# A hybrid decoder step on one core: the first two expert units expert by expert, ring places freed one by one, zero products ahead of the last up

## The chip, the cores and the metric

The kernel runs on one core of one Trainium2 chip. The metric is the device time of one execution in microseconds (us), given as the median of several runs. The engines are named as in the profile: PE (TensorE, the matrix products), PEld (its weight loads), DVE (VectorE), ACT (ScalarE), POOL (GpSimd) and SP (SyncE, which here only issues DMAs). DMAs are issued on three queues, those of SP, ACT and POOL, and are carried by the same 16 DMA engines.

## The reference

One inference step of a one-layer decoder, all in float32, for a prompt of 512 tokens and 8 decode tokens of width 1024. Two groups of attention heads (stick-breaking and NSA) read one input projection, are normalised and go through an output projection into the residual x. Behind them stands the part that matters here, a mixture of experts:

```python
def hierarchical_moe(h, ...):                       # h: 520 rows of 1024
    g_idx = argmax(group logits)                    # one of 4 groups
    top_w, top_i = lax.top_k(softmax(expert logits of that group), 2)
    expert_id = g_idx * 4 + top_i                   # two of 16 experts per row
    gate = einsum('nd,edf->nef', h, w_gate)         # 1024 -> 512 for each expert
    up   = einsum('nd,edf->nef', h, w_up)
    act  = silu(gate) * up * combine                # combine is zero for experts not chosen
    return einsum('nef,efd->nd', act, w_down)       # 512 -> 1024
# then: output = rms_norm(x + moe(rms_norm(x)), norm_final)
```

Each of the 16 experts has three weight matrices of 2 MB (gate, up, down), 96 MB in all.

## The kernel before

**Rows by expert.** The kernel computes for each expert only the rows that chose it. The normalised rows are written to DRAM (h_rows), each row gets a slot in a table, and the rows of an expert are gathered from DRAM by an indirect DMA on POOL, turned on PE, and multiplied by the expert's weights. Work is cut into 16 units (`UNITS`). Units 0 and 1 are special: they hold rows of experts 1 and 2 (`FIXED`), of which 64 rows each are known before the last tile of the prompt (unit 0) and 32 rows each come with the last tile (unit 1). Units 2 to 15 are one expert each with 32 to 128 rows, in an order of experts that is computed on the chip (`order_i`) and read by SP into registers.

**A unit's steps.** On PE: gate products (8 blocks of K, `gate_or_up(j, 0)`), up products, the turning of the activations (`transpose_acts`), down products (`finish_down`), and between them the rows of the next unit (`rows_of`). On ACT: exp of the gate, the copies of the turned rows and activations, the copy of the output (`y_out`) and its store (`store_rows`). On DVE: the rest of silu (`gated`), the product with up (`times_up`), half of the copies. The two units use separate banks for gate and up (`hidden_to`). Behind unit 2's up, DVE also computes where each row's results will lie (`extra_blocks`, `place_results`), a chain of small operations.

**The stream of weights.** 48 loads of 2 MB (`CHUNKS`) go through a ring of 8 places (`RING`, `homes`). SP issues them in the order of `CHUNKS`: gate 0, gate 1, up 0, up 1, down 0, down 1, gate 2, up 2 (the first eight, at fixed points of the plan, as soon as the attention part no longer needs the space), then gate 3, up 3, down 2, gate 4, up 4, down 3 and so on. The eight first ones are issued in the order 0, 1, 3, 4, 2, 5, 6, 7. Load n of the ring waits until load n - 8 has been used, by a count that PE raises at the end of a whole gate, up or down (`e_gate`, `e_up`, `e_down`). Since units 0 and 1 both read experts 1 and 2, the counts wait for unit 1 for both places (`max(j, 1) + 1`). In this text "gate 7" is the load or the product group of unit 7. A DMA that stands in SP's queue behind a waiting one waits too.

**The plan.** A recording layer writes the kernel as a list of steps (`PLAN`), and each engine takes its own steps in that order. In the attention part the order comes from times in units that `place(time, step)` gives (`agenda`); behind it the order is written out by hand. `fill(n)` puts n of the 16 steps of unit 0's gate products between the last steps of routing on PE.

**The output.** The results of experts go to DRAM (`expert_rows`), those of units 14 and 15 stay on chip. For each of the five tiles (order `SUM_ORDER`: 0, 4, 1, 2, 3; 4 is the tile of 8 decode rows) DVE adds the two gathered rows to x (`add_rows`, two operations, the second writes into a pair of PSUM banks that PE has "opened" with products of zeros), PE adds the late units' rows by products with selection matrices, ACT takes squares and the root, DVE scales (`scaled`), and SP stores. There are three pairs of banks (`final_banks`): tiles 0 and 2 share banks 3 and 4, tile 3 and the decode tile share 6 and 7, tile 1 has 0 and 1. So tile 2 must wait for tile 0's scaling and tile 3 for the decode tile's.

## Time and profile before

| what | us |
|---|---|
| median of 3 runs (753.1 to 756.13) | 754.16 |
| the profiled execution | 759.51 |
| its span, from the first to the last instruction | 757.7 |
| PE busy | 699.8 |
| DVE busy | 343.3 |
| ACT busy | 215.9 |
| mean granted clock of TensorE | 0.973 of full |

The span covers all but 1.8 us of the profiled execution, and this execution is 5.4 us longer than the median. Times in the rows are us from the start of the span. A row of the timeline gives start, length, engine, line, operation, tile written and tiles read, count; in square brackets stands how long the engine was idle before it and what it then waited for. Rows that end in "xN" merge N instructions. Before about 250 us lie the input projection and the decode tokens, up to some 465 us the prompt's attention, and from there the experts.

### The profile page before, as it was taken

Reading aid. Unit: us, or ns where it says so; the run is one execution under the profiler, and the core shown is the slowest. Engines: PE = TensorE matmul, PEld = TensorE weight load, DVE = VectorE, ACT = ScalarE, POOL = GpSimd, SP = SyncE. Lnnn points to the kernel's source line nnn. Section 1 sums busy time; section 2 is a strip of 40 time slices with the busy share of each in tenths; the row PEclk is TensorE's granted clock in tenths of the full one; section 3 lists DMA queues with packets and bytes.
Section 4 is the critical chain, followed back from the end, with each engine's and each line's share of the span. In section 5 each row is a group of like instructions: output and inputs, shape, how many; then the busy total and the mean of one; then the engine's idle time right before and its main releaser. Section 6 shows DMA issues by size and latency. Waiting matters only on the chain.

```text
span 757.7 us, 13582 instructions
## 1 busy us (share of the span) xinstructions
PE 699.8 (92%) x5251; PEld 385.2 (51%) x5251; DVE 343.3 (45%) x770; ACT 215.9 (28%) x557; POOL 125.4 (17%) x174
## 2 busy tenths in 40 slices
PE   7878999999999989979989999999899999989885
PEld 3446456444554445545545665745554664565331
DVE  6411103595222455665775665606634253123245
ACT  1111111112211555657657831011010110101103
POOL 0111100120000443142253241110010000100050
PEclk9998999999999989999999999999999999999988
DMA  8265891667757530000000069999999999999982
GB/s 290 72 181 158 237 395 44 230 233 231 230 175 209 202 132 1 1 3 1 1 29 1 1 221 384 309 383 396 365 396 397 395 408 398 376 404 408 410 288 112
DMA packets 101491, 172.55 MB, mean 228 GB/s; under 512 B 22893, under 2 KB 40653, under 8 KB 101394
## 3 DMA queue, kind: packets, MB, share of 16 engines
q1 hardware_dynamic: 79682, 142.83, 52.6%
q10 hardware_dynamic: 18656, 20.35, 7.9%
q0 software_dynamic: 3088, 8.49, 3.2%
q8 instruction: 43, 0.70, 0.4%
q14 instruction: 22, 0.18, 0.1%
HBM read 151.78 MB, written 22.98 MB: 231 GB/s over the span
## 4 chain that ended last, share of the span: by engine, by line
PE 70%; issue 9%; DVE 7%; DMA 6%; ACT 4%; SPq 2%; POOL 2%; DVEq 0%; ACTq 0%; POOLq 0%
PE bank L2701 15%; PE bank L3168 13%; PE bank L1998 7%; PE bank L2731 6%; PE bank L3151 6%; PE bank L1915 3%; PE bank L1936 3%; DMA reg<-w_up 3%; DMA reg<-w_gate 3%; PE bank L1794 2%; PE bank L1949 2%; SPq L2211 2%; PE bank L3172 1%; PE bank L1917 1%; DMA x<-x_prompt 1%
## 5 line engine op out<-in xcount | busy, mean ns | idle before, releaser
L3168 PE MATMUL bank<-reg 128*128 128x512 f32 (+1 forms) x352 | 148.4, 568 | 0.8 <-DMA reg<-w_in 0.4
L2701 PE MATMUL bank<-reg,qreg 128*32 128x128 f32 (+2 forms) x1264 | 109.2, 336 | 6.6 <-DMA reg<-w_up 3.9
L3168 PEld LDWEIGHTS bank<-reg 128*128 128x128 f32 x352 | 65.3, 194 | 59.3 <-issue 55.5
L2701 PEld LDWEIGHTS bank<-reg,qreg 128*32 128x32 f32 (+2 forms) x1264 | 66.3, 126 | 47.8 <-issue 30.6
L1280 POOL TENSOR_SCALAR reg<-reg,st,gates 128x128 f32<-128x128 f32 (+3 forms) x64 | 41.2, 652 | 185.2 <-DVE st L1568 185.1
L3151 PE MATMUL bank<-cf,reg 128*128 128x128 f32 (+1 forms) x384 | 61.9, 280 | 10.0 <-DVE rt L1759 4.9
L1998 PE MATMUL bank<-reg 128*128 128x512 f32 x128 | 62.7, 613 | 0.4 <-DVE x L1680 0.3
L3151 PEld LDWEIGHTS bank<-cf,reg 128*128 128x128 f32 (+1 forms) x384 | 41.9, 142 | 30.2 <-issue 24.0
L3002 ACT ACTIVATE work<-bank 128x128 f32<-128x128 f32 (+5 forms) x107 | 40.8, 411 | 49.2 <-PE bank L3151 47.8
L2731 PE MATMUL bank<-reg,work 128*32 128x256 f32 (+1 forms) x368 | 47.5, 476 | 1.1 <-ACT work L2353 0.7
L1564 DVE TENSOR_REDUCE st<-bank 128x2 f32<-128x256 f32 (+3 forms) x32 | 26.3, 822 | 41.8 <-PE bank L1917 41.7
L3106 DVE COPY work<-bank 128x128 f32<-128x128 f32 (+4 forms) x55 | 22.8, 429 | 49.3 <-PE bank L3151 49.3
L2292 POOL DMA_INDIRECT work<-h_rows,ids x14 | 13.6, 969 | 176.6 <-PE bank L2744 128.1
L1395 ACT ACTIVATE reg<-bank,st 128x128 f32<-128x128 f32 (+3 forms) x64 | 33.2, 524 | 28.8 <-DVE st L1564 28.6
L1936 PE MATMUL bank<-work,vreg 128*64 128x128 f32 x480 | 38.0, 289 | 2.0 <-DVE work L3106 2.0
L2969 POOL TENSOR_TENSOR reg<-reg,cf 128x128 f32<-128x128 f32 (+5 forms) x30 | 15.4, 533 | 146.7 <-ACT reg L3059 138.8
L2459 DVE TENSOR_SCALAR work<-work 128x256 f32<-128x256 f32 (+3 forms) x16 | 5.4, 335 | 74.6 <-ACT work L2348 74.6
L1936 PEld LDWEIGHTS bank<-work,vreg 128*64 128x64 f32 x480 | 26.0, 139 | 24.3 <-issue 21.8
L2460 DVE RECIPROCAL work<-work 128x256 f32<-128x256 f32 (+3 forms) x16 | 36.0, 2253 | 0.6
L2361 ACT COPY work<-bank 128x512 f32<-128x512 f32 (+1 forms) x16 | 8.9, 558 | 78.8 <-PE bank L2731 58.5
L1998 PEld LDWEIGHTS bank<-reg 128*128 128x128 f32 x128 | 22.1, 193 | 16.8 <-issue 15.8
L2731 PEld LDWEIGHTS bank<-reg,work 128*32 128x32 f32 (+1 forms) x368 | 16.9, 122 | 26.3 <-issue 20.3
(374 smaller groups left out, 921.9 us busy)
## 6 DMA issues: line engine op xcount, KB each, us to landing
reg<-w_gate SPq DMA_DIRECT2D x13, 2048.0 KB, 19.2
reg<-w_down SPq DMA_DIRECT2D x12, 2048.0 KB, 20.3
reg<-w_up SPq DMA_DIRECT2D x11, 2048.0 KB, 18.3
reg<-w_in ACTq DMA_DIRECT2D x16, 512.0 KB, 6.6
expert_rows<-vreg SPq DMA_DIRECT2D x14, 512.0 KB, 6.9
vreg<-w_up SPq DMA_DIRECT2D x3, 2048.0 KB, 18.8
reg<-cache_sb_k SPq DMA_DIRECT2D x16, 256.0 KB, 4.5
reg<-cache_sb_v SPq DMA_DIRECT2D x16, 256.0 KB, 3.9
```

What stands on the lines that cost most here:

```text
L1280: ins = G.tensor_scalar(prob, prob, w[:, e:e + 1], gate[:, e:e + 1], ALU.mult, ALU.mult)
L1395: nc.scalar.activation(prob_of(key, e)[:, 0:n], at(ring, key)[:, 0:n], ACT.Exp, bias=st[:, top:top + 1], accum_out=st[:, col:col + 1]).the ...
L1564: V.tensor_reduce(st[:, top:top + 2], psum[:, 2:4, 0:n], AX.X, ALU.max, negate=True).then_inc(sg["arg"], 1)
L1936: ins = T.matmul(to[64 * e:64 * e + 64, :], v, probT[:, turn_at[key] % 3, e, k * P:(k + 1) * P], start=(k == 0 and b != WIN), stop=(k == i ...
L1998: ins = T.matmul(at(ring, ("wout", i, group))[0:r, :], chunks_of(i)[:, part, 0:r], w_out[group // 2][:, k, 512 * half:512 * half + 512], s ...
L2460: link_loop(V.reciprocal(s_, s_), 3 * j + 2)
L2701: ins = T.matmul(to[rows, at_:at_ + w], rowsT[b][:, k, r0:r0 + n], w_[:, k, h * w:(h + 1) * w], start=(k == 0), stop=(k == KD - 1))
L2731: ins = T.matmul(to[rows, at_:at_ + w], actsT[j % 2][:, 4 * r0 // P + k % per, q:q + n], w_[:, k, w * h:w * h + w], start=(k == 0), stop=( ...
L3002: ins = nc.scalar.activation(dst, src, ACT.Copy, scale=scale)
L3106: ins = nc.vector.tensor_copy(dst, src)
L3151: ins = nc.tensor.transpose(dst, src, ident[0:src.shape[0], 0:src.shape[0]])
L3168: ins = nc.tensor.matmul(at("m", ("proj", n))[:, 0:w], hT[:, k, i * P:(i + 1) * P], win[:, pos % 2, k, 0:w], start=(k == 0), stop=(k == KD ...
```

## The change

Four things change.

1. **The order of loads.** Up 1 (load 3) is placed in the agenda, ahead of the store of h rows behind which it stood. Up 2 (load 7) is split: 4 and 2 of its 8 K blocks go right behind gate 2, the remaining 2 at the old place. Down 2 now stands ahead of gate 3 in the ring, and a table `USED` tells which load's place each load takes (`HOME`).
2. **Units 0 and 1.** Unit 1's gate products (`late_gate`) go into the middle and the end of unit 0's (`fill(6)`, expert 1's block of unit 1, `fill(4)`, expert 2's block), up and down go expert by expert over both units, and the counts rise by one after each expert of unit 1, so that a place is freed as soon as both units have used it (`freed`). Unit 0's counts rise at the end of unit 0 (`finished(0)` is 2). The order of experts is computed behind the gates. Unit 1's down products go to bank 1, its activations are turned in the middle of the downs, and the turns of unit 2's rows stand between the last two down blocks.
3. **Zero products.** Ahead of the last up (up 15), PE does ten products of zeros into the banks of tile 0.
4. **The output.** Four pairs of banks (tile 0: 6 and 7, tile 1: 4 and 5, tile 2: 2 and 3, decode tile: 0 and 1): only tile 3 waits for a pair, tile 0's, and this wait stands on PE ahead of tile 2's products. DVE adds four tiles before the first scaling. Two pairs are opened before down 15 and two behind it.

On SP the order of DMAs around the attention's end, before and after (`h2_rows` is the store of h rows, in brackets what a DMA waits for; `L1256` and `L1266`, `L2211` and `L2239` or `L2242` are the same line in both):

```order
L1256 DMA h2_rows<-reg1 128x1024 [waits h2] x2
L2211 DMA qreg<-w_up 128x8x512 [waits z_full]
L2211 DMA reg0<-w_down 128x4x1024 [waits t_full]
L1256 DMA h2_rows<-reg1 128x1024 [waits h2]
L2211 DMA vreg<-w_up 128x8x512 [waits st_v,pv]
L2211 DMA reg0<-w_down 128x4x1024 [waits m_full]
L2211 DMA reg1<-w_gate 128x8x512 [waits m_full]
L2211 DMA reg1<-w_up 128x8x512 [waits st_h2,e_rowsT_full]
```

```order
L1266 DMA h2_rows<-reg1 128x1024 [waits h2]
L2239 DMA qreg<-w_up 128x8x512 [waits z_full]
L1266 DMA h2_rows<-reg1 128x1024 [waits h2]
L2239 DMA reg0<-w_down 128x4x1024 [waits t_full]
L1266 DMA h2_rows<-reg1 128x1024 [waits h2]
L2239 DMA vreg<-w_up 128x8x512 [waits st_v,pv]
L2239 DMA reg0<-w_down 128x4x1024 [waits m_full]
L2239 DMA reg1<-w_gate 128x8x512 [waits m_full]
L2242 DMA reg1<-w_up 128x4x512 [waits squares]
L2242 DMA reg1<-w_up 128x2x512
L2242 DMA reg1<-w_up 128x2x512 [waits st_h2,e_rowsT_full]
L2239 DMA reg1<-w_down 128x4x1024 [waits e_gate]
```

Up 1 (`qreg<-w_up`) moves past one store, up 2 (`reg1<-w_up`) comes in three pieces, and a down (down 2) stands ahead of the read of the order.

On PE the first two units, from the last 16 fill rows (`64x256` into `L2050`/`L2060` are unit 0's gate) to the first down block, before and after. `32x128` are unit 1's blocks, `64x256` unit 0's:

```order
L2050 MATMUL bank<-reg0,qreg 64x256 x15
L2676 MATMUL bank<-gain,token 1x16 [waits turns,x_dve]
L2701 MATMUL bank<-reg1,qreg 32x128 [waits z_dve,o_act,ga_act,t_dve,gb_act,e_rows_a,m_dve,e_rows_v,slot0]
L2701 MATMUL bank<-reg1,qreg 32x128 x31
L2701 MATMUL bank<-reg0,qreg 32x128 [waits slot1]
L2701 MATMUL bank<-reg0,qreg 32x128 x31
L2701 MATMUL bank<-vreg,qreg 64x256 [waits slot2]
L2701 MATMUL bank<-vreg,qreg 64x256 x15
L2701 MATMUL bank<-qreg 64x256 [waits slot3]
L2701 MATMUL bank<-qreg 64x256 x15
```

```order
L2060 MATMUL bank<-reg0,qreg 64x256 x7
L2711 MATMUL bank<-reg1,qreg 32x128 [waits o_act,z_dve,t_dve,ga_act,gb_act,m_dve,e_rows_a,e_rows_v]
L2711 MATMUL bank<-reg1,qreg 32x128 x31
L2060 MATMUL bank<-reg0,qreg 64x256 x8
L2711 MATMUL bank<-reg0,qreg 32x128 x32
L2727 MATMUL bank<-gain,token 1x16 [waits turns,x_dve]
L2711 MATMUL bank<-vreg,qreg 64x256 [waits o_act,t_dve,z_dve,ga_act,m_dve,gb_act,slot2]
L2711 MATMUL bank<-vreg,qreg 64x256 x15
L2711 MATMUL bank<-vreg,qreg 32x128 x32
L2711 MATMUL bank<-qreg 64x256 [waits slot3]
```

Unit 1's gates have moved into and behind unit 0's, ahead of the product that gives the order (`gain,token`), and unit 1's up of an expert follows unit 0's of the same.

Further on PE, from the first turning of activations to unit 2's gate (`64x512` is a down block of unit 0, `32x256` one of unit 1, `cf,work 128x128` are turns):

```order
L2707 MATMUL bank<-cf,work 128x128 [waits e_act]
L2707 MATMUL bank<-cf,work 128x128 x3
L2731 MATMUL bank<-reg0,work 64x512 [waits slot4,e_actT]
L2731 MATMUL bank<-reg0,work 64x512 x7
L2731 MATMUL bank<-reg0,work 64x512 [waits slot5]
L2731 MATMUL bank<-reg0,work 64x512 x7
L2707 MATMUL bank<-cf,work 128x128 [waits e_act]
L2707 MATMUL bank<-cf,work 128x128
L2683 MATMUL bank<-cf,work 128x128 [waits e_x0]
L2683 MATMUL bank<-cf,work 128x128 x7
L2731 MATMUL bank<-reg0,work 32x256 [waits e_y_v,slot4,e_y_a,e_actT]
L2731 MATMUL bank<-reg0,work 32x256 x15
```

```order
L2758 MATMUL bank<-cf,work 128x128 [waits e_act]
L2758 MATMUL bank<-cf,work 128x128 x3
L2781 MATMUL bank<-reg0,work 64x512 [waits e_actT,slot4]
L2781 MATMUL bank<-reg0,work 64x512 x7
L2758 MATMUL bank<-cf,work 128x128 [waits e_act]
L2758 MATMUL bank<-cf,work 128x128
L2781 MATMUL bank<-reg0,work 32x256 [waits e_actT]
L2781 MATMUL bank<-reg0,work 32x256 x15
L2781 MATMUL bank<-reg0,work 64x512 [waits slot5]
L2781 MATMUL bank<-reg0,work 64x512 x7
L2734 MATMUL bank<-cf,work 128x128 [waits e_x0]
L2734 MATMUL bank<-cf,work 128x128 x7
```

Unit 1's turns and its first down block stand between unit 0's two down blocks, with a wait for ACT's copy (`e_actT`) that nothing separates from the turns.

The diff, cut to its core:

```diff
-OPEN_FIRST = (0, 4, 1)
+OPEN_FIRST = (0, 4)
 CHUNKS = [("gate", 0), ("gate", 1), ("up", 0), ("up", 1), ("down", 0), ("down", 1), ("gate", 2), ("up", 2)]
-CHUNKS += [(w, j - (w == "down")) for j in range(3, 15) for w in ("gate", "up", "down")]
+CHUNKS += [("down", 2), ("gate", 3), ("up", 3)]
+CHUNKS += [(w, j - (w == "down")) for j in range(4, 15) for w in ("gate", "up", "down")]
 CHUNKS += [("gate", 15), ("down", 14), ("up", 15), ("down", 15)]
+USED = list(CHUNKS)
+USED[RING:RING + 3] = [("gate", 3), ("up", 3), ("down", 2)]
+HOME = {key: n for n, key in enumerate(CHUNKS[:RING])}
+for n, key in enumerate(CHUNKS[RING:]):
+    HOME[key] = HOME[USED[n]]
...
+    place(SHARE * (REP * 2 + 5) + 269, step, "chunk", 3)
     for _, _, f, args in sorted(agenda):
         f(*args)
-    for n in (3, 4):
-        step("chunk", n)
+    step("chunk", 4)
...
-    step("chunk", 7)
+    step("chunk_part", 7, 1)
     use("x", ("count",), "dve")
     step("count")
     sg.mark("turns", 0)
-    fill(10)
+    fill(6)
+    step("late_gate", 0)
+    fill(4)
+    step("late_gate", 1)
...
+        elif kind == "late_gate":
+            e, = key
+            if e == 0:
+                acquire_all(pe)
+                pe.wait_ge(sg["e_rows_a"], 1)
+                pe.wait_ge(sg["e_rows_v"], 1)
+            two_blocks(1, 0, e).then_inc(sg["e_gate"], 1)
...
-        n = (3, 0, 3, 6, 6)[i]
+        n = (6, 4, 2, 6, 0)[i]
...
+    def finished(j):
+
+        return j + 2
+
+    def freed(j):
+
+        return j + 2 if j else 1
...
             for n in range(RING, len(CHUNKS)):
+                before, j = USED[n - RING]
+                if CHUNKS[n] == ("gate", 3):
+                    sg.wait(sp, "x_dve", ("order",))
                 if CHUNKS[n][0] == "gate":
                     next_expert(CHUNKS[n][1])
-                before, j = CHUNKS[n - RING]
-                sp.wait_ge(sg["e_" + before], max(j, 1) + 1)
+                sp.wait_ge(sg["e_" + before], freed(j))
                 load_chunk(sp, n, expert_reg[CHUNKS[n][1]])
...
-            for i in (0, QT, 1):
+            for i in (0, QT, 1, 2):
                 add_rows(i)
             sg.wait(dve, "gain_in", "final")
             scaled(0)
-            add_rows(2)
-            scaled(QT)
             add_rows(3)
-            for i in range(1, QT):
+            for i in (QT, 1, 2, 3):
                 scaled(i)
...
+            wait_chunk(pe, "up", 0)
+            two_blocks(0, 1, 0)
+            two_blocks(1, 1, 0).then_inc(sg["e_up"], 1)
+            wait_chunk(pe, "up", 1)
+            two_blocks(0, 1, 1).then_inc(sg["e_up"], 1)
             sort_ids()
-            gate_or_up(1, 1, sg["e_up"])
+            two_blocks(1, 1, 1).then_inc(sg["e_up"], 1)
             pe.wait_ge(sg["e_act"], 1)
             transpose_acts(0, 4, sg["e_actT_full"])
-            finish_down(0)
+            wait_chunk(pe, "down", 0)
+            pe.wait_ge(sg["e_actT"], 1)
+            down_block(0, 0)
             pe.wait_ge(sg["e_act"], 2)
             transpose_acts(1, 4 * UNITS[1] // P, sg["e_actT_full"])
+            pe.wait_ge(sg["e_actT"], 2)
+            down_block(1, 0).then_inc(sg["e_down"], 1)
+            wait_chunk(pe, "down", 1)
+            down_block(0, 1).then_inc(sg["e_down"], 1)
             rows_of(2)
-            finish_down(1)
+            down_block(1, 1).then_inc(sg["e_down"], 1)
...
+                if j == 2:
+                    pe.wait_ge(sg["e_y_a"], 2)
                 gate_or_up(j, 1, sg["e_up"])
...
+            pe.wait_ge(sg["picked"], TILES)
+            for _ in range(5):
+                zero_banks(0, True, True)
             gate_or_up(LAST, 1, sg["e_up"])
...
+            for i in (1, 2):
+                open_banks(i).then_inc(sg["late_full"], 1)
             for i in SUM_ORDER:
                 to = final_banks(i)
-                if i not in OPEN_FIRST:
-                    sg.wait(pe, "final", (0, QT)[i - 2])
-                    open_banks(i).then_inc(sg["late_full"], 1)
+                if i == 2:
+                    sg.wait(pe, "final", 0)
+                    open_banks(3).then_inc(sg["late_full"], 1)
```

## Rows read from the trace of the kernel before

**Rows 1.** Page, its span and the DMA share in 40 slices (tenths).
```profile
span 757.7 us, 13582 instructions
...
DMA  8265891667757530000000069999999999999982
```

**Rows 2.** Windows: length, busy us of PE to POOL, clock, DMA share, GB/s.
```profile
480.00:540.60 60.60, 56.73 (x552) 32.19 (x542) 32.41 (x86) 5.94 (x12) 5.52 (x6) 1.00 1.04 377
540.60:673.70 133.10, 133.10 (x1363) 75.24 (x1363) 47.99 (x86) 15.56 (x35) 8.61 (x9) 1.00 1.04 395
673.70:735.50 61.80, 53.42 (x482) 27.87 (x480) 17.29 (x21) 5.58 (x13) 9.92 (x10) 0.92 1.00 384
```

**Rows 3.** Timeline of SP's queue, 370 to 560 us.
```profile
383.98 57.15 SPq L1256 DMA_DIRECT2D h_rows<-reg  x2
441.17 0.43 SPq L2211 DMA_DIRECT2D qreg<-w_up  x1
...
476.07 0.37 SPq L2211 DMA_DIRECT2D reg<-w_up  x1
...
483.29 0.39 SPq L2211 DMA_DIRECT2D reg<-w_gate  x1
...
552.21 0.37 SPq L2211 DMA_DIRECT2D reg<-w_gate  x1
```

**Rows 4.** Line L2211's issue to landing: whole span; 430-480; 514-560; down 15.
```profile
DMA to landing us min/median/max: 9.3/19.9/25.8
...
DMA to landing us min/median/max: 10.5/13.2/14.6
...
DMA to landing us min/median/max: 16.0/18.3/21.0
...
reg<-w_down SPq DMA_DIRECT2D x1, 2048.0 KB, 25.4
```

**Rows 5.** Timeline of PE, 428 to 500 us.
```profile
429.40 0.29 PE L1917 MATMUL bank<-cb 128*128 128x128 bf16 x2
...
474.77 4.54 PE L2050 MATMUL bank<-reg,qreg 128*64 128x256 f32 x40
...
479.37 3.70 PE L2701 MATMUL bank<-reg,qreg 128*32 128x128 f32 x128
...
495.34 7.09 PE L2731 MATMUL bank<-reg,work 128*64 128x512 f32 x32 [0.68 <-ACT work L2353]
```

**Rows 6.** Timeline of PE at unit 4's gate.
```profile
540.59 5.56 PE L2701 MATMUL bank<-qreg 128*64 128x256 f32 x96 [2.60 <-DVE qreg L2451]
```

**Rows 7.** Timeline of PE, units 13 to 15.
```profile
675.80 7.23 PE L2701 MATMUL bank<-reg,qreg 128*64 128x256 f32 x96 [2.09 <-DMA reg<-w_gate]
...
683.43 5.56 PE L2701 MATMUL bank<-reg,qreg 128*64 128x256 f32 x96
...
699.09 3.67 PE L2701 MATMUL bank<-vreg,qreg 128*64 128x256 f32 x32
...
704.76 5.52 PE L2731 MATMUL bank<-qreg,work 128*64 128x512 f32 x48 [1.36 <-DMA qreg<-w_down]
...
714.72 3.65 PE L2731 MATMUL bank<-reg,work 128*64 128x512 f32 x16 [0.46 <-DMA reg<-w_down]
722.24 5.36 PE L2701 MATMUL bank<-reg,qreg 128*64 128x256 f32 x32 [3.87 <-DMA reg<-w_up]
...
728.56 1.65 PE L2661 MATMUL bank<-cb,wr 32*128 32x512 bf16 x6
730.15 5.35 PE L2731 MATMUL bank<-reg,work 128*64 128x512 f32 x16
```

**Rows 8.** Output: line L2634's first and last start; timeline of PE and DVE.
```profile
L2634 DVE SCALAR_TENSOR_TENSOR x<-reg,weight,x x4: 1264/1272/1286, 729.6 to 744.9; 128x1024 f32<-128x1024 f32 x4
...
743.89 1.95 PE L2840 MATMUL bank<-work,cf 64*128 64x512 f32 x4 [1.45 <-DVE bank L2638]
...
753.28 1.28 DVE L2644 SCALAR_TENSOR_TENSOR x<-bank,small,gain 128x1024 f32<-128x1024 f32 x1 [1.42 <-ACT small L2416]
```

94 lines of the change are left out of this document (60 added, 34 removed).

## The prediction

> **What bounds the kernel now.** The page comes first, for the shares: PE is at 92%, and the DMA row stands at 9 from the 25th slice on in all but the last two [rows 1]. Both look full there, so the windows tell which one is: from 480 to 735 us the 16 DMA engines are busy all the time (share 1.00 to 1.04, 377 to 395 GB/s), while PE has no gap at all from 540.6 to 673.7 and gaps of 8.4 us in 673.7 to 735.5 [rows 2]. So the expert weights (48 loads of 2 MB, in one fixed order on SP's queue) and PE run side by side, both full in the middle, and the stream of loads decides at the end: PE waits 2.09 us for gate 13, 1.36 for down 13, 0.46 for down 14 and 3.87 for up 15 [rows 7], 7.8 of the 8.4 together. Two of these waits are followed by products at half clock: 96 products take 7.23 us after the first and 5.56 otherwise, 32 take 5.36 after the last and 3.67 otherwise, and the last down takes 5.35 where down 14's like group took 3.65 [rows 7]. Then 22.2 us of output sums follow up to 757.7, in which DVE and PE take turns [rows 1, 8].
>
> Then the start of the stream. SP stands from 383.98 to 440.80 on a store of h rows, and up 1 goes out only behind it, at 441.17 [rows 3], although the score products whose end it waits for ended at 429.7 [rows 5]. Up 2 goes out at 476.07, gate 3 at 483.29. And how long a load takes: 10.5 to 14.6 us from 430 to 480, where the queue is short, 16.0 to 21.0 from 514 to 560, where others stand ahead of it; the least of all, gate 1's at the start on idle engines, was 9.3 [rows 4].
>
> **Part 1: loads earlier.** Up 1 goes ahead of the store: 429.8 instead of 441.17. Up 2 goes in three pieces: 1.5 MB waits only for the squares of the last tile's mixture, long done when SP comes from gate 2 (about 465), and 0.5 MB waits for what all of it waited for, 476.07. What is queued on SP behind that wait, down 2, isn't ready sooner anyway. Down 2 takes gate 0's place, which is free after 12 of the 16 fill steps and unit 1's gate block of expert 0: fills cost 0.45 us each and the block 1.85 [rows 5], so 474.77 + 2.7 + 1.9 = 479.4, against 483.29 for the first load from the ring before. Gate 3 needs the order, which now comes behind all gates: 483.1 + 0.2 and the register load, about 484.7. Up 3 goes at 488.9, gate 4 at 494.2, up 4 at about 502, down 3 at about 508.
>
> What is that worth? A load lands at the later of two times: 5.1 to 5.9 us behind the one ahead of it (395 GB/s with the stores and gathers between), or its issue plus the time that a load alone takes. Followed so, the stream stands 8 to 10 us earlier at units 3 and 4. But a place comes free only when PE has used it, and PE isn't earlier. The tightest point is gate 7: it was issued at 552.2, right when its place came free, and landed 16.0 us later, the least in [rows 4] for this stretch. Alone it needs 9.3 to 13.2 us (ends: the shortest of all, and the median before 480). I take 10, nearer to the low end, because before 480 stores and indirect transfers stood between, and 0.7 for PE's own delay (part 2): 16.0 - 10 - 0.7 = 5.3, with the loads around it at 5 to 7. Behind that the engines are full again and can't catch up, so **the end of the stream moves by 5.5 us** (2 to 8): up 15 from 722.2 to 716.7, down 15 (issued at 703.9, 25.4 us) from 729.3 to 723.8 [rows 4, 7].
>
> The Trainium skill (DMA: Bandwidth & Descriptors, Anatomy of one DMA) fits a DMA as 2.0 us plus its bytes at 436 GB/s, 6.8 us for 2 MB, for the gpsimd path. The shortest of this trace is 9.3, on SP's queue; by the page's figure the stream would move by 8.5 us, and the second rival below would be the likeliest.
>
> **Part 2: the first two units.** The same products in another order. Gates, ups and turns add to the same 474.77 to 494.01, since no load is waited for (down 0 and 1 landed long before). Then down of unit 0, expert 0 (3.55), turns of unit 1 (0.4), and here is a new wait: ACT must copy these turns before unit 1's down can start. The same hand-over for unit 0 costs PE 0.68 us with a copy of 512 columns [rows 5]; with 256 columns I take 0.5. Before, it was covered by the rows of unit 2. Another 0.2 for the rest: **PE is 0.7 us late** at unit 2 (0.3 to 1.2). Unit 0's exponential and gating come some 2 us later on ACT and DVE; up of both experts is done at 492.4, DVE is free by then, and PE wants its result at 494.0. DVE's long chain of placing results starts behind up 2 and ends at 540.59, where PE waits 2.60 us for it [rows 6]; it moves with PE, so the 0.7 isn't absorbed there. The gather for unit 2 starts 2 us later and its rows are wanted at 505. Up 2 also waits for unit 1's output to be copied out of its bank: ACT gets there behind unit 0's stores, at 510, and PE comes at 515. The branch for more rows stays untaken.
>
> **Part 3: the end of the experts.** PE reaches gate 13 at 673.7 + 0.7 = 674.4; it has landed at 670.2. No wait, and full clock: from there to down 13 PE needs the 27.6 us of before less the lost 1.7, so down 13 starts at 700.3 and ends at 705.8 instead of 710.3. Down 14 ends at 713.4. Ten zero products take 0.21 to 0.27 us each (six take 1.65 in [rows 7]): 2.6 us at most, up to 716.0. They lie in the wait for up 15, which lands at 716.7; cover gone, they would cost 2.6. Up 15 takes 3.67, DVE's product and its turns 1.0, four opening products 1.0: 722.4. Down 15 lands at 723.8, and its products at full clock end 3.65 later: **727.5, before 735.5**.
>
> **Part 4: the output.** With four pairs of banks only tile 3 waits for a pair, tile 0's. Counted from the end of down 15, PE and DVE alone would need 17.6 us instead of 22.2: the waits for opened banks, of which 1.45 us stands in [rows 8], and the products at half clock go. That gives 745.1. But DVE has a limit of its own. Its first add waits for the gathered rows, 729.6 now [rows 8]; the gathers wait for unit 13's stores, so they move with down 13, by 4.5 us: 725.1. From there DVE has no gap: four pairs of adds at 2.5 us to 735.1, one scaling to 736.4, the last pair to 738.9 (PE's opening and tile 2's products, behind this scaling, end at 739.0 beside it); then the last tile's products 2.1, squares and root on ACT 1.75, scaling 1.3: 744.1, and 3.1 us for the last store as now (753.28 + 1.28 to 757.7). **End at 747.3**.
>
> So the span falls from 757.7 to 747.3, by 10.4 us; the profiled execution of 759.51 would be 749.1. Its span and frame stand 5.4 us above the median of 754.16, so the same 10.4 from the median give 743.8; I say **744.0**.
>
> **Rivals.** *The stream gains little* (0 to 3 us), because loads alone take 13 to 16 us or the splitting of up 2 costs what it brings. For it: loads took 10.5 to 14.6 us before 480 with few in flight [rows 4]. At no shift the zeros still keep the clock up for up 15, down 15's products end at 733.0, DVE's adds start at 729.6 as now, and the end is 751.8. At 3 us gate 13 costs nothing, down 13 1.3, the adds start at 726.4 and the end is 748.6. Gain 5.9 to 9.1: 745.1 to 748.3.
>
> *The stream gains 8 us or more*, and PE is the bound. Down 15 then starts at 722.4 without a wait and ends at 726.1; gathers on freer engines land 1 to 3 us sooner, and the end is 743.7 to 745.7, gain 12 to 14: 740.2 to 742.2.
>
> *No change that can be measured*: the last 22 us stay as they are, because products between idle times run at half clock. In [rows 8] the first half of tile 2's products took 1.95 instead of 1.13 and the tile 1.65 more than others; three such tiles cost 4.9 us, which eats the 4.6 of part 4, and with a stream that gains nothing only the 2.5 us of down 15 (735.5 to 733.0) remain: 751.7.
>
> *Slower*: the queue runs dry. From unit 3 on each load is issued only when its place is free, with nothing queued ahead, and pays its whole time alone. That is nothing new as long as this time is under the 16.0 us of gate 7; each us above, less PE's 0.7, moves the whole stream back by one. The 5.9 us that are left at no shift pay for the first ones, so it decides from 21.2 us on, and at 25.0 us the time is 758. Against it: no load with a short queue took over 14.6.
>
> **How the numbers follow.** Forecast 0.60, little gain in the stream 0.17, PE as the bound 0.16, no change 0.05, slower 0.02. The range takes the first three: 740.8 to 748.5. Half a percent is 3.8 us, about what a measurement of this kernel can tell from none; faster by more than that 0.93, within 0.05, slower 0.02.
>
> **What would show it.** Up 1 issued near 430; the first ring load near 479.5; a wait of about 0.5 us ahead of unit 1's down block; gate 4 of PE 0.7 us later than 540.6; no wait at gate 13 and none at down 13, 96 products in 5.5 us each time; down 15 landing near 724; DVE without a gap from its first add near 725 up to the last. Wrong if a PE wait of over 1 us appears between 480 and 670 beside DVE's chain, if gate 13 is still waited for, or if DVE's adds still start at 729.

## The result, and the profile after

The changed kernel takes 751.01 us (median of 13 runs, 746.94 to 754.5), the kernel before 754.56 beside it (13 runs): ratio 0.9938, 95% interval 0.9914 to 0.9961. So it is faster, but by 0.6% only: 4.7 us by the ratio (3.6 between the medians), where 10.4 were forecast, and 751.0 lies above the range of 740.8 to 748.5. On another chip the same kernel gave 749.73 against 758.07, ratio 0.9885 (0.9844 to 0.9926) [e5 below]. Ratios are of the fast runs alone; the medians of e1, e14 and e16 below still hold 3, 3 and 1 slow runs and are up to 0.8 us above those of their fast runs.

The profiled execution has the median's time, 751.01; its span is 749.2 where the prediction had 747.3. In this kernel L2239 issues whole loads and L2242 the pieces of up 2, L2060 is a fill, L2711 a block of units 0 and 1, L2752 gate or up, L2781 and L2742 down, L2698 products of zeros, L2914 the late products, L2673 and L2677 DVE's adds, L2683 its scaling. The page's span and DMA share, then the windows (columns as in [rows 2]) over the start, PE's stretch without a gap, and the end:

```profile
span 749.2 us, 13606 instructions
...
DMA  8266890677658530000000059999999999999995
```
```profile
480.00:542.94 62.94, 57.23 (x508) 31.03 (x505) 32.83 (x90) 6.70 (x13) 5.52 (x6) 1.00 1.02 363
542.94:677.68 134.74, 134.74 (x1363) 76.27 (x1363) 48.00 (x86) 15.59 (x35) 8.61 (x9) 0.99 1.03 392
677.68:729.30 51.62, 50.08 (x492) 26.14 (x488) 13.61 (x18) 5.59 (x13) 8.04 (x8) 1.00 1.00 386
```

PE's idle time behind 677.68 is 1.5 us, where [rows 2] had 8.4: the waits for loads are gone. But PE arrives there 4 us later than before. SP's queue, against [rows 3]:

```profile
428.85 0.38 SPq L2239 DMA_DIRECT2D qreg<-w_up  x1
...
463.80 10.28 SPq L2242 DMA_DIRECT2D reg<-w_up  x3
478.66 0.37 SPq L2239 DMA_DIRECT2D reg<-w_down  x1
483.67 0.39 SPq L2239 DMA_DIRECT2D reg<-w_gate  x1
...
556.25 0.37 SPq L2239 DMA_DIRECT2D reg<-w_gate  x1
```

The start is as forecast (429.8, 479.4, 484.7). Gate 7 is not: issued at 556.25 where 552.9 was forecast, it took 9.5 us and landed at 565.8, only 2.4 before the 568.2 of the kernel before. PE, against [rows 5 to 7]:

```profile
473.90 2.81 PE L2060 MATMUL bank<-reg,qreg 128*64 128x256 f32 x24
...
488.84 0.73 PE L2711 MATMUL bank<-vreg,qreg 128*32 128x128 f32 x17 [1.31 <-issue]
...
501.22 5.52 PE L2781 MATMUL bank<-reg,work 128*32 128x256 f32 x48 [0.46 <-ACT work L2391]
...
509.55 14.00 PE L2752 MATMUL bank<-reg,qreg 128*128 128x512 f32 x32
...
542.94 7.25 PE L2752 MATMUL bank<-qreg 128*64 128x256 f32 x96 [2.59 <-DVE qreg L2490]
...
677.68 5.56 PE L2752 MATMUL bank<-reg,qreg 128*64 128x256 f32 x96
...
703.55 5.52 PE L2781 MATMUL bank<-qreg,work 128*64 128x512 f32 x48
...
716.98 2.33 PE L2698 MATMUL bank<-cb,wr 32*128 32x512 bf16 x10
719.64 3.67 PE L2752 MATMUL bank<-reg,qreg 128*64 128x256 f32 x32 [0.33 <-DMA reg<-w_up]
...
725.66 3.65 PE L2781 MATMUL bank<-reg,work 128*64 128x512 f32 x16 [0.26 <-DMA reg<-w_down]
```

From the first fill step to unit 2's gate it takes 35.65 us; before it was 32.4. A gap of 1.31 us stands inside the up products in which PE waits for nothing that the profile shows, and unit 4's gate ran in part at half clock (7.25, not 5.56; granted clock 0.50 from 543.3 to 546.7). The output, against [rows 8], is DVE's chain with no gap but 0.24 us ahead of its last scaling:

```profile
727.14 1.28 DVE L2673 SCALAR_TENSOR_TENSOR x<-reg,weight,x 128x1024 f32<-128x1024 f32 x1 [3.28 <-DMA reg<-expert_rows,y_slots]
...
744.78 1.28 DVE L2683 SCALAR_TENSOR_TENSOR x<-bank,small,gain 128x1024 f32<-128x1024 f32 x1 [0.24 <-ACT small L2455]
```

### The profile page after: what moved, and what is told of

It is laid out like the page before. It is cut to its first block, busy times and chain, and to the rows that moved or that the text cites. A ratio compares the mean times of both kernels' runs of the same rounds, so it can differ in the third digit from the quotient of the medians.

```text
span 749.2 us, 13606 instructions
## 1 busy us (share of the span) xinstructions
PE 697.4 (93%) x5261; PEld 382.9 (51%) x5261; DVE 343.3 (46%) x770; ACT 216.3 (29%) x557; POOL 125.5 (17%) x174
## 4 chain that ended last, share of the span: by engine, by line
PE 71%; DVE 7%; SPq 6%; issue 6%; ACT 4%; DMA 4%; POOL 0%; ACTq 0%; DVEq 0%
PE bank L2752 15%; PE bank L3242 13%; PE bank L2008 7%; PE bank L3225 6%; PE bank L2781 6%; SPq L1191 4%; PE bank L1946 3%; PE bank L1925 3%; PE bank L1804 2%; PE bank L2711 2%; PE bank L1959 2%; PE bank L2742 2%; DMA pages<-page_table 2%; PE bank L3246 1%; PE bank L2060 1%
## 5 line engine op out<-in xcount | busy, mean ns | idle before, releaser
L3242 PE MATMUL bank<-reg 128*128 128x512 f32 (+1 forms) x352 | 146.8, 562 | 1.2 <-DMA reg<-w_in 0.8
L2752 PE MATMUL bank<-reg,qreg 128*32 128x128 f32 (+2 forms) x1072 | 100.1, 340 | 0.9 <-ACT qreg L2380 0.6
L2752 PEld LDWEIGHTS bank<-reg,qreg 128*32 128x32 f32 (+2 forms) x1072 | 59.3, 126 | 39.6 <-issue 25.1
L2008 PE MATMUL bank<-reg 128*128 128x512 f32 x128 | 65.0, 632 | 0.4 <-DVE x L1690 0.3
L2781 PE MATMUL bank<-reg,work 128*32 128x256 f32 (+1 forms) x336 | 44.2, 475 | 1.8 <-ACT work L2391 1.6
L1946 PEld LDWEIGHTS bank<-work,vreg 128*64 128x64 f32 x480 | 25.4, 137 | 24.4 <-issue 21.9
L3133 ACT COPY reg<-bank 128x512 f32<-128x512 f32 (+1 forms) x20 | 10.9, 547 | 62.4 <-PE bank L3242 62.4
```

Source lines behind the costliest of these rows:

```text
L1946: ins = T.matmul(to[64 * e:64 * e + 64, :], v, probT[:, turn_at[key] % 3, e, k * P:(k + 1) * P], start=(k == 0 and b != WIN), stop=(k == i ...
L2008: ins = T.matmul(at(ring, ("wout", i, group))[0:r, :], chunks_of(i)[:, part, 0:r], w_out[group // 2][:, k, 512 * half:512 * half + 512], s ...
L2752: ins = T.matmul(to[rows, at_:at_ + w], rowsT[b][:, k, r0:r0 + n], w_[:, k, h * w:(h + 1) * w], start=(k == 0), stop=(k == KD - 1))
L2781: ins = T.matmul(to[rows, at_:at_ + w], actsT[j % 2][:, 4 * r0 // P + k % per, a0:a0 + n], w_[:, k, w * h:w * h + w], start=(k == 0), stop ...
L3242: ins = nc.tensor.matmul(at("m", ("proj", n))[:, 0:w], hT[:, k, i * P:(i + 1) * P], win[:, pos % 2, k, 0:w], start=(k == 0), stop=(k == KD ...
```

## A ruler for single executions

One profile can't be set against another by its span alone: the attention part ends up to 4 us earlier or later whatever the kernel. But three marks are in each: PE's wait of 1.17 us for DVE near 445 us (M; 1.16 to 1.18 in all), the first fill step (F) and DVE's first add of gathered rows (A). From M to F, F to A, and A to the end (us), the span, and the median with its ratio to the kernel before on the same chip:

| kernel | M-F | F-A | A-end | span | median | ratio [95%] |
|---|---|---|---|---|---|---|
| before | 28.85 | 254.8 | 28.1 | 757.7 | | |
| before (e1) | 29.65 | 253.7 | 26.7 | 753.7 | 757.09 | 0.9988 [0.9947, 1.0029] |
| before (e16) | 29.04 | 253.2 | 25.4 | 753.6 | 759.88 | 1.0038 [0.9993, 1.0082] |
| new output alone (e2) | 32.45 | 254.6 | 22.1 | 753.2 | 755.31 | 1.0007 [0.9981, 1.0033] |
| the same (e14) | 34.48 | 253.8 | 22.1 | 754.5 | 755.41 | 0.9961 [0.993, 0.9993] |
| output and zeros (e13) | 35.50 | 256.2 | 22.1 | 759.5 | 756.98 | 0.9999 [0.9967, 1.0031] |
| up 1 early alone (e17) | 28.85 | 251.5 | 26.0 | 750.3 | 753.63 | 0.9962 [0.9932, 0.9992] |
| up 1 early and output (e18) | 28.86 | 252.9 | 22.0 | 751.5 | 751.71 | 0.9947 [0.9918, 0.9976] |
| changed, old output (e6) | 28.85 | 252.3 | 27.6 | 752.7 | 752.2 | 0.9919 [0.9883, 0.9955] |
| changed, old output, no zeros (e15) | 28.85 | 252.4 | 26.9 | 752.2 | 753.75 | 0.9965 [0.9934, 0.9997] |
| changed | 28.85 | 253.2 | 22.1 | 749.2 | 751.01 | 0.9938 [0.9914, 0.9961] |
| changed (e5) | 28.86 | 252.6 | 22.1 | 748.9 | 749.73 | 0.9885 [0.9844, 0.9926] |
| changed, no zeros (e3) | 28.85 | 251.7 | 22.1 | 749.8 | 749.68 | 0.9907 [0.9873, 0.994] |
| before, half loads (e4) | 32.36 | 243.6 | 24.8 | 745.4 | 747.09 | 0.9892 [0.9843, 0.9941] |
| changed, half loads (e8) | 28.85 | 249.8 | 22.1 | 745.8 | 746.44 | 0.9853 [0.9798, 0.9908] |
| changed, unit by unit (e7) | 28.85 | 252.1 | 22.0 | 747.5 | 750.99 | 0.9921 [0.9888, 0.9953] |
| changed, quiet queue (e9, one run) | 28.85 | 251.6 | 22.1 | 747.2 | 748.99 | |
| changed, rows earlier, no zeros (e10) | 28.85 | 255.3 | 22.0 | 750.8 | 752.57 | 0.9966 [0.9941, 0.9991] |
| changed, ups by unit, rows earlier (e11) | 28.85 | 255.8 | 22.0 | 751.0 | 754.84 | 1.0007 [0.9988, 1.0027] |
| changed, late starts (e12) | 28.85 | 252.1 | 22.0 | 748.4 | 751.82 | 0.9952 [0.9924, 0.998] |

Each row is one profile, while the median and the ratio stand for many executions. The unaltered kernels (three profiles of before, two of changed) differ by up to 1.6 us from F to A, so smaller differences there show nothing.

## Experiments on the kernel before

**e1 and e16: the kernel before, unaltered.** No edit.

> The kernel before once more, unchanged, for a second look at where its time goes. Theory A (the profiled execution of before was one with unusually long waits at the end): PE's waits for gate 13, down 13, down 14 and up 15 sum to 3 to 5 us instead of 7.8, the span is 750 to 754. Theory B (the waits are the same in every execution, and the change lost its gain elsewhere): they sum to 7 to 8.5 us again and the span is 752 to 758.

> The kernel before, unaltered, for one more profile of it on the same chip: 280 to 283 us from the first fill step to the end by theory A, with 26.5 to 28.2 us from DVE's first add; ratio 0.997 to 1.003. Rival B (the two profiles of it so far were both long by chance): 277 to 279 us.

Measured: spans of 753.7 and 753.6, 4 us under the first profile's 757.7. Neither waits for gate 13, and both write most of the output at full clock (A-end 26.7 and 25.4 against 28.1). PE's waits for down 13, down 14 and up 15 sum to 5.8 and 5.9 us, where the first profile had 7.8 with gate 13: between theory A and theory B of e1. From F to the end it is 280.4 and 278.6 us, so e16 falls to its rival B. In e1 the wait for up 15 is the old one:

```profile
718.74 6.58 PE L2701 MATMUL bank<-reg,qreg 128*64 128x256 f32 x32 [3.88 <-DMA reg<-w_up]
```

So part of what the prediction set out to remove (2.09 us at gate 13, 1.7 of half clock behind it, 1.65 in tile 2) is in some executions only: e2 and e13, with the old loads too, wait 1.31 and 1.23 us for gate 13. How much of it stands in a median these runs don't show, for e1's and e16's profiled executions (755.5 both) lie below the medians of their own runs.

**e2, e14, e13: the output alone, and with the zero products.** On the kernel before, only:

```diff
-        n = (3, 0, 3, 6, 6)[i]
+        n = (6, 4, 2, 6, 0)[i]
...
-            for i in (0, QT, 1):
+            for i in (0, QT, 1, 2):
                 add_rows(i)
```

with the openings and waits that belong to it; e13 also has the ten products ahead of up 15.

> The kernel before with part 4 of the change alone: four pairs of banks, DVE adding four tiles before the first scaling, two pairs opened behind the last down; no zero products, old order of loads and units. If DVE's chain of adds from its first gathered rows bounds the output (my prediction): from the first add to the end of the span 22.1 us instead of 28.1, but counted from the end of down 15 (735.5 before) some 16 to 17.6, so 4.5 to 5.5 us faster than before, ratio 0.993 to 0.994. If the output were bound by PE's opening products and half clock, less than 2 us, ratio over 0.997.

> Part 4 alone on the kernel before, a second time. Theory A: 276 to 278.5 us from the first fill step to the end, ratio 0.993 to 0.998. Rival B: ratio 0.998 to 1.003.

> The kernel before with the new output and the zero products, old loads and old first two units. Theory A (the output carries most of the gain, as the profiles say: from the first fill step to the end the kernel before takes 280.4 to 282.9 us, with the new output alone 276.7, the changed one 274.7 to 275.3): 275.5 to 278 us from the first fill step to the end, 22.1 us from DVE's first add to the end, ratio 0.993 to 0.998. Rival B (the output gives nothing in the time, as the median of the first run of it said): ratio 0.998 to 1.003, and 280 us or more from the first fill step.

Measured: A to end is 22.1 us in all three, 3.3 to 6.0 shorter than in the three profiles of the kernel before, as part 4 wants it. Yet the medians hardly move (ratios 1.0007, 0.9961, 0.9999). In the three profiles the gain is lost ahead of the experts: M-F is 32.45 to 35.50. In e14 first POOL, then PE:

```profile
458.92 0.99 POOL L2281 DMA_INDIRECT work<-h_rows,first_ids  x1 [7.70 <-issue]
```
```profile
466.40 1.16 PE L2038 MATMUL bank<-cf,work 128*128 128x128 f32 x8 [0.97 <-DMA work<-h_rows,first_ids]
...
468.32 3.68 PE L2051 MATMUL bank<-reg,qreg 128*64 128x256 f32 x16 [0.51 <-ACT qreg L2336]
```

PE waits 0.97 us for the gather of the first rows (unit 0's), and then runs at half clock for 13.7 us (granted clock 0.50; 16 products in 3.68, else 1.95). The kernel before does the same work with a wait of at most 0.2 us in two of its profiles and 0.73 in e1: its gather goes out at M + 13.06 to 14.50, in these three at M + 14.73 to 15.63. The new output need not be the reason: e4 below, whose edit begins only with the loads of unit 4 at 497 us, has the gather at M + 15.51, a wait of 1.75 us and an M-F of 32.36. The late gather comes with the old start in some executions; how often, and so whether it explains the medians, isn't shown.

**e17 and e18: up 1 early, alone and with the output.** The edit of e17, and e18 is e2 with it:

```diff
+    place(SHARE * (REP * 2 + 5) + 269, step, "chunk", 3)
     for _, _, f, args in sorted(agenda):
         f(*args)
-    for n in (3, 4):
-        step("chunk", n)
+    step("chunk", 4)
```

> The kernel before with up 1 alone issued ahead of the store of h rows (near 429 us); nothing else. Theory A (the store of h rows at +4.57 us lands sooner when up 1's 2 MB no longer stand ahead of it, so the gather of the first rows goes out by +10.7 us instead of +13.1 to +15.6, counted from PE's wait of 1.17 us near 445, and PE never waits for it): first fill step at +28.85, where the kernel before and those with its loads had 28.86 to 35.5; behind it 278.6 to 282.9 us as before; ratio 0.994 to 0.998. Rival B (the place of the fill steps varies by chance of the execution): gather at +13 us or later in it, first fill step anywhere from 28.9 to 32.5, ratio 0.998 to 1.002.

> Part 4 and the early up 1 on the kernel before; old places, old first two units, no zero products. Theory A (early up 1 guards the first rows, the output is 4.6 us shorter, the rest of the stream brings 1 to 2 us): first fill step at +28.85, behind it 275.8 to 278 us, ratio 0.990 to 0.995, within 2 us of the changed kernel. Rival B (places freed singly carry the gain): ratio 0.996 to 1.000.

Measured: theory A in both as to the gather and the ratio (from F to the end it is 277.5 and 274.9 us, 1 us less than A's ranges). POOL's gather in e17 and in the changed kernel:

```profile
454.34 0.99 POOL L2278 DMA_INDIRECT work<-h_rows,first_ids  x1 [3.35 <-DVE first_ids L1737]
```
```profile
455.16 0.99 POOL L2316 DMA_INDIRECT work<-h_rows,first_ids  x1 [3.07 <-DVE first_ids L1747]
```

It goes out at M + 10.4 (it waits for its row numbers alone), PE never waits for it, and F stands at M + 28.85. By the code the gather also waits until the store of h rows has landed, a moment that the profile doesn't show. Before, this store (issued at M + 4.57 in all) stood behind up 1 and down 0 in one queue; with up 1 issued 11.4 us sooner its 2 MB have landed by then (in the changed kernel 12.4 us ahead of the store's issue, in the kernel before 1.2 behind it). One moved load gives ratio 0.9962, with the output 0.9947, and from F to the end e18 takes 274.9 us, the changed kernel 275.3 and 274.7. **These two edits alone come near to what the whole change does**, and the loads and first units alone, early up 1 with them (e15 below, 0.9965), are no faster than e17. Two things stay open. The changed kernel has 0.9938 in the result but 0.9885 in e5 and 0.9907 without zeros (e3), on other chips, so that 2 us of the median or more may come from the rest. And e12 below, with up 1 late again, has 0.9952: in the changed kernel early up 1 isn't shown to be needed.

**e4: half the bytes of each load of units 4 to 15** (the output differs), on the kernel before:

```diff
+        if j >= 4:
+            k = (FF // P if kind == "down" else KD) // 2
+            sp.dma_start(chunk(kind, j)[:, 0:k, :], src[:, 0:k, :]).then_inc(sg[f"slot{n % RING}"], 16)
+            return
```

> The kernel before with only half the bytes of every load of the experts of units 4 to 15 (the other half of the weights in these places is what lay there), so the output is not the reference's; every product, wait and copy stays. It shows what the stream of loads costs. If the loads decide only at the end (PE full from 540.6 to 673.7): the waits of 7.8 us, the half clock behind them (5 us) and the contention of the gathers go, 10 to 13 us faster, ratio 0.983 to 0.987. If PE is slowed by the loads in another way too, more than 15 us.

Measured: 747.09 us, ratio 0.9892 (0.9843 to 0.9941), a little less gain than expected. No wait for a load is left; F-A is 243.6, so the loads cost the kernel before 9.6 to 11.3 us there. The profile has 3.5 us of the late gather ahead of F. POOL's gather, PE's wait for it and DVE's first add in e4:

```profile
460.15 0.99 POOL L2282 DMA_INDIRECT work<-h_rows,first_ids  x1 [8.46 <-issue]
```
```profile
467.63 1.09 PE L2037 MATMUL bank<-cf,work 128*128 128x128 f32 x8 [1.75 <-DMA work<-h_rows,first_ids]
```
```profile
720.56 1.28 DVE L2638 SCALAR_TENSOR_TENSOR x<-reg,weight,x 128x1024 f32<-128x1024 f32 x1 [1.31 <-DMA reg<-expert_rows,y_slots]
```

## Experiments on the changed kernel

**e5: unaltered. e8: with the half loads of e4.**

> The changed kernel, unaltered. Theory A (PE loses about 3 us in the first two units, not 0.7, and the end of down 15 moves by 6 us): ratio to before 0.992 to 0.996, PE again has an unexplained gap near 488 us with a wait of about 0.5 us ahead of unit 1's down block, and unit 2's gate group starts 2 to 3.5 us later behind the start of the fill steps than the 32.4 us of before. Rival B (the 3 us were one execution's bad luck): the gap is absent, unit 2's gate group starts 0.5 to 1.2 us later, and the ratio is 0.986 to 0.990.

> The changed kernel with half the bytes of each load of units 4 to 15 (the output is another for it): what PE, DVE and ACT need when no load is waited for. The same cut made the kernel before 747.1 us (0.989 of it). Theory A (PE is late in the first two units by 3 us and the output gains 2 to 4): 745 to 748, ratio 0.986 to 0.991, so the changed kernel stands only 3 to 6 us above its own floor without loads. Rival B (the loads still hold the changed kernel): 741 to 744, 0.981 to 0.984.

Measured: e5 again has the gap (0.66 us) and the wait (0.46), and 35.0 us from F to unit 2's gate, which is theory A; its ratio is the one that rival B forecast. e8 gives 746.44 us, 0.9853 (0.9798 to 0.9908). PE reaches gate 13 202.9 us behind F in e8 and in e5 (676.81 and 677.09), with half the bytes as with all: between unit 2 and down 14 the changed kernel doesn't wait for loads at all. There PE alone sets the time; behind it e5 needs 2.8 us more than e8 (from F to the end 274.7 us in e5, 271.9 in e8). Against e4's, its own floor is no lower (746.44 and 747.09), and behind F it is higher: 271.9 us where e4 has 268.4. The output gives 2.7 us, but the first units (2.6), the zeros (2.3 without a cover here) and unit 4's gate in part at half clock in this profile (1.5) take more.

**e9: a quiet queue.** Down 2 and gate 3 are cut to a sixteenth and an eighth (the output differs).

> The changed kernel with down 2 and gate 3 loaded to an eighth (gate) and a sixteenth (down) only, so that the DMA engines are nearly idle from 480 to 488 us (the output is another for it). Theory A (the gap of 0.4 to 1.3 us behind the 79th product of up 0 and up 1 is PE waiting for its code: a 16 KB packet of the instruction queue starts 2.2 to 2.5 us before PE goes on, and it comes late because the weight loads fill the engines): the gap is gone or under 0.2 us, and the packet comes earlier relative to the block's start than the 3.4 to 4.1 us of now. Rival B (the code is asked for too late by PE itself): the gap stays at 0.4 to 1.3 us and the packet stays 3.4 us or more behind the block's start.

Measured: theory A, in one execution, whose time is not compared. The block of e9 without a gap, and the packet of the instruction queue (packets, MB, share of 16 engines in a window of 0.1 us from 482.0), then that of the changed kernel (from 486.5):

```profile
482.00 5.56 PE L2715 MATMUL bank<-vreg,qreg 128*64 128x256 f32 x96
```
```profile
q8 instruction: 1, 0.02, 60.0%
```
```profile
q8 instruction: 1, 0.02, 60.2%
```

Such a packet takes 0.96 us of one engine. How late it starts behind the block's first product sets the gap: 0.0 us (e9) and 1.6 (e12) none; 2.7 (e10) none, but the block takes 5.79 us instead of 5.56; 3.2 (e6, e15) 0.38; 3.4 (e5), 3.5 (e3) and 3.6 (e8) 0.66; 4.2 (changed) 1.31. PE goes on 2.2 to 2.4 us behind its start. In e7 below it starts 3.3 us in as well, and no gap follows: there the block's first 64 products are the long ones, and the 79th comes only 7.7 us in, not 4.8. So PE starves for code, and e9 says that the packet is late because the weight loads fill the engines. Why it is early in e12, whose engines are as full, isn't known. The Trainium skill (Runtime: NRT & Kernel Launch, Instruction fetch mechanics) says that code comes in blocks of 16 KiB over a DMA queue of the sequencer and that this is mostly hidden; the packet agrees, the hiding doesn't hold here.

**e7: ups and downs of the first two units unit by unit. e11: only the ups.** e7's edit on PE (e11 keeps the downs by expert, with unit 2's rows moved as in e10):

```diff
-            two_blocks(1, 1, 0).then_inc(sg["e_up"], 1)
             wait_chunk(pe, "up", 1)
-            two_blocks(0, 1, 1).then_inc(sg["e_up"], 1)
+            two_blocks(0, 1, 1).then_inc(sg["e_up"], 2)
             sort_ids()
+            two_blocks(1, 1, 0)
```

> The changed kernel with up and down of the first two units computed unit by unit again, the old order on PE (the places of up 0 and down 0 come free later for it). Theory A (the order by experts costs PE some 2 us): unit 2's gate group starts 1.5 to 2.5 us earlier than in the changed kernel, the gap near 488 us is gone, while gate 3 and up 3 go out 1 to 4 us later; the time is within 1.5 us of the changed kernel either way. Rival B (the gap on PE comes from the DMA queue beside it, not from the order): the gap stays, unit 2's gate group starts within 0.7 us of the changed kernel's.

> The changed kernel with up of the first two units unit by unit (the place of up 0 comes free one block later, that of up 1 as now), down by experts as changed, unit 2's rows earlier as in e10, zero products kept. Theory A (PE's lateness sits in the ups by experts, 1.5 to 2.2 us with the gap; up 3 goes out 3.5 us later, gate 4 as now): from the fill steps to unit 2's gate group 32.9 to 33.3 us instead of 35.0 to 35.7, no gap near 488 us, gate 13 of PE 1 to 2 us earlier, and the time 0 to 2 us under the changed kernel's. Rival B (the stream gives it back, as with unit-by-unit ups and downs): DMA waits of 2 us or more together at gate 13 to up 15, the time within 0.7 us of the changed kernel's.

Measured in e7: no gap, 32.8 us from F to unit 2's gate, so the order by experts costs 2.2 to 2.85 us. And PE's gain is given back at once, to waits for loads at the end:

```profile
679.40 5.56 PE L2752 MATMUL bank<-reg,qreg 128*64 128x256 f32 x96 [0.68 <-DMA reg<-w_up]
...
700.54 5.52 PE L2781 MATMUL bank<-qreg,work 128*64 128x512 f32 x48 [1.17 <-DMA qreg<-w_down]
...
718.08 5.36 PE L2752 MATMUL bank<-reg,qreg 128*64 128x256 f32 x32 [1.62 <-DMA reg<-w_up]
```

750.99 us, 0.9921 (0.9888 to 0.9953), beside 749.73 (e5) on the same chip with an interval that overlaps. Down 13 ends 232.6 us behind F, 1.7 to 2.6 sooner than in the changed kernel and e5, but the span ends 274.1 behind it, only 0.6 to 1.2 sooner. PE and the stream are in balance there; that places freed singly are worth the delay of PE isn't to be seen. e11 waits 3.81 us in front of the rows' turns, as e10 does, and takes 754.84, 1.0007 (0.9988 to 1.0027).

**e10: unit 2's rows earlier, no zeros.**

```diff
+            rows_of(2)
             pe.wait_ge(sg["e_actT"], 2)
             down_block(1, 0).then_inc(sg["e_down"], 1)
...
-            rows_of(2)
```

> The changed kernel with the turns of unit 2's rows between the turns of unit 1 and unit 1's first down block, and without the zero products. Theory A (the wait of 0.46 us for ACT's copy is the only cost that this place has, and each us of PE up to gate 7 counts): no wait there, the stretch from the turns of unit 0 to unit 2's gate group is 13.7 to 13.9 us instead of 14.24, the time 0.3 to 1 us under the changed kernel's. Rival B (unit 2's rows aren't there yet): PE waits 0.5 to 2 us for the gather in front of the rows' turns, and the time is the changed kernel's or up to 1.5 us more.

Measured: rival B, and worse than it said:

```profile
502.39 1.09 PE L2734 MATMUL bank<-cf,work 128*128 128x128 f32 x8 [3.41 <-DMA work<-h_rows,ids]
```

The 0.46 us are gone and 3.41 come instead; 752.57 us, 0.9966 (0.9941 to 0.9991). PE comes to unit 2 3.2 to 3.9 us later than in the changed kernel, and the median is 1.6 to 2.9 us above those of the changed kernel and of e3.

**e12: up 1 and up 2 at their old points.** The calls of the old order, all places as changed.

> The changed kernel with up 1 issued behind the store of h rows again (near 441) and up 2 whole near 475; all other orders and places as changed. Theory A (the gain comes from places that are free sooner, not from the early start of up 1 and up 2: the stream's tightest point is the place of gate 7): gate 7 issued and landed within 0.7 us of the changed kernel's against the start of the fill steps, time within 1 us of it, ratio to before 0.988 to 0.995. Rival B (the early starts carry it): gate 7 lands 1.5 to 3 us later, DMA waits of 3 us or more at the end, ratio 0.995 to 1.0.

Measured: gate 7 goes out at 555.01, 80.8 us behind F (82.4 and 81.4 in the changed kernel), and lands 90.3 behind it (91.9, 90.7). 751.82 us, 0.9952 (0.9924 to 0.998). Theory A as to the stream, though the ratio is a hair over its range: the earlier starts don't reach gate 7, since a load there waits for its place, and this place even comes free 0.7 to 1.6 us sooner, because PE has no gap here (34.05 us from F to unit 2's gate). The gather went out at M + 12.65, still in time, so what early up 1 guards against didn't happen in this profile.

**e6, e15, e3: the changed kernel with the old output, with neither new output nor zeros, without zeros alone.** The diffs are those above, reversed.

> The changed kernel with the output of before (two pairs of banks less, the old order of DVE's sums); loads, first two units and zero products stay. Part 4 alone brought nothing on the kernel before. Theory A (part 4 pays only when the gathered rows and down 15 are early, as they are here): slower than the changed kernel by 2 to 4 us, ratio to before 0.997 to 1.001. Rival B (part 4 brings nothing anywhere, all of the gain is the stream's): within 1 us of the changed kernel, 0.992 to 0.996.

> The changed loads and first two units alone: the output of before, and no zero products. Theory A (these parts bring 1 to 4 us, the output the rest): 278 to 281 us from the first fill step to the end, 26.5 us or more from DVE's first add to the end, ratio 0.994 to 0.999. Rival B (the stream carries the gain): 275 to 277 us, ratio 0.988 to 0.993.

> The changed kernel without the ten zero products ahead of up 15. In the trace of the changed kernel they end at 719.3 and up 15's load lands at 719.6, so they lie in a wait. If they only keep the clock up: a wait of 2.6 us ahead of up 15, up 15 and down 15 perhaps at half clock, 0 to 3.4 us slower than the changed kernel. If they cost time (where the load is early): 0 to 2 us faster. I expect 0 to 1 us slower than the changed kernel, ratio to before 0.993 to 0.996.

Measured: with the old output 752.2 us beside 749.73 (e5), as theory A had it, though the ratio of 0.9919 lies in rival B's range; A to end is 27.6 (e6) and 26.9 (e15, theory A, 279.3 us from F to the end). The wait for an opened pair is back in e6:

```profile
737.64 1.13 PE L2915 MATMUL bank<-work,cf 64*128 64x512 f32 x4 [1.45 <-DVE bank L2677]
```

The intervals of e5 and e6 overlap; the 2.5 us stand on the medians and on these rows. Without zeros (e3) the time is 749.68, no slower: up 15 then waits 3.21 us and takes 5.36, but DVE's adds, which set the end, start no later. The zeros did not hold the clock reliably either: behind them up 15 took 3.67 in five profiles of nine (the changed kernel, e8, e9, e12, e13) and 5.36 in four, so in e5 after a wait of 0.54.

## Why the prediction was right or wrong

**From the execution to the median: wrong, and the largest error.** The forecast for the changed execution was 749.1, and the median of the changed kernel is 751.0, so the working was 1.9 us off. It was off by more and had luck: F came 0.9 us earlier than in the profile that it started from, and from F to the end it gave 272.5 us where 275.3 were measured. The other 5.1 come from taking the full 10.4 off a median which lay 5.4 below the profiled execution. 10.4 contained 2.1 us of wait at gate 13 and the half clock behind it and in tile 2, which e1 and e16 have not.

**Part 1, the stream: right in its times, and the term that failed in its worth.** Up 1, down 2 and gate 3 went out within 1.0 us of the forecast, gate 4, up 4 and down 3 1.2 to 1.7 us behind it. Gate 7 was rightly named as the tightest point, and its load took 9.5 (forecast 10). But its place came free 3.3 us later than forecast (556.25, not 552.9), and the end of the stream (down 15's landing) moved by 3.8 us, from 729.3 to 725.5, not 5.5. Most of the 3.8, too, belongs to this pair of executions: counted from F, down 15 lands at 254.5, 252.5 and 252.9 us in the three profiles of the kernel before and at 251.6 in both of the changed one, gate 7 at 93.4, 90.6 and 92.5 against 91.9 and 90.7. **So where the sum had 5.5 us, the repeats show 0.9 to 2.9**, and e17, with the old ring, lands down 15 at 250.5. Down 15 from issue to landing in the changed kernel (issued at 701.05) and in e1 (at 700.41, F at 473.30):

```profile
reg<-w_down SPq DMA_DIRECT2D x1, 2048.0 KB, 24.5
```
```profile
reg<-w_down SPq DMA_DIRECT2D x1, 2048.0 KB, 25.4
```

The places come free when PE has used them, and PE was later than part 2 had it. e12 shows that the early starts did nothing for the stream. What early up 1 did do in e17, guarding the gather of the first rows, stands in no step of the prediction; the first profile showed no wait there, and the 0.7 us of margin weren't looked at. The shortest 2 MB load of the profile before was also not gate 1's 9.3 us, but the 8.5 of `reg<-w_out`.

**Part 2: the other mis-sized term.** "0.7 us late (0.3 to 1.2)" measured 3.2 us, 2.6 in e5. The wait for ACT was right (0.46 against 0.5). That the ups "add to the same" was wrong: from the first fill step to the first turns PE needs 21.4 us (20.8 in e5) instead of 19.2, gap included. From there to unit 2's gate it needs 14.2 instead of 13.2, 1.1 more where 0.7 was forecast. Unit 4's gate in part at half clock (1.7) came on top in this profile; e1 and e16 have it too in the old kernel, so it isn't the change's. The gap of 1.31 us is the wait of over 1 us between 480 and 670 that the prediction named as a sign of being wrong.

**Part 3: the waits went, the gain didn't come.** No wait at gate 13 nor at down 13, as forecast. But down 13 ended at 709.1, 1.2 us earlier and not 4.5, since PE was late: measured from F it is 235.2 us (234.3 in e5), where the forecast had 231.0 and the kernel before 235.5, 233.5 and 233.7. The 4.2 us are the 2.5 of part 2 and the 1.7 of unit 4's gate. PE has gained nothing there; the waits only became work done later. That the zeros keep the clock up for up 15 came true here, but in five profiles of nine only. Down 15 ended at 729.3 (forecast 727.5, before 735.5).

**Part 4: right in the profile.** 19.9 us from the end of down 15 (forecast 19.8), DVE's adds without a gap, 22.05 from the first add. The add came at 727.1, not 725.1, as it hangs on down 13, and the end with it. In the medians of the kernel before (e2, e14, e13) the worth of this part didn't show.

**The rivals.** The outcome is nearest to *the stream gains little* (2.4 us at gate 7, 3.8 at the end), though its time, 745.1 to 748.3, was missed too and the reason was another: not long loads, but PE, which frees the places. PE as the bound, forecast for a stream that gains 8 us, came with one that gained 3.8. The queue did not run dry; the output kept its gain.

## What to carry to other kernels

Before taking a gain off a median, look whether the waits that it removes are in a second profile of the same kernel; where an execution is above its median, its surplus can be just those waits. Compare profiles from a common mark, not from the start of the span. In a ring of buffers a place comes free when the consumer has used it, so an earlier start of the stream is worth nothing behind the point where loads wait for places, and a consumer that is late (3.2 us here) moves the ring. Look also at what else hangs on a queue: in e17 the load that was moved paid, by the rows, not by landing sooner itself but by letting a small store, and a gather behind it, through.

## What the runs showed of the hardware

Code is a transfer like others: with the 16 engines full of 2 MB loads, a 16 KB packet of the instruction queue that started over 3 us into a dense run of small products left PE idle for 0.38 to 1.31 us at the same instruction each time (six profiles), and with the engines nearly idle (e9, one profile) for none. And what a short wait costs depends on the clock behind it. At the same point, PE's wait for the first rows, 0.73 us (e1) was followed by full clock; 1.89 (e2) and 1.75 (e4) by 16 products in 3.60 and 3.63 us instead of 1.95; 1.51 (e13) and 0.97 (e14) by 17.1 and 13.7 us at half clock (granted clock 0.50), which with the wait itself taken off made F 5.1 and 4.7 us later. The length of the wait doesn't tell which. The window of e14 at half clock (columns as in [rows 2]):

```profile
467.30:480.90 13.60, 13.09 (x69) 8.93 (x69) 6.67 (x37) 1.73 (x6) 1.92 (x2) 0.50 0.73 200
```
